# A hybrid block with 256 tokens: 32 tokens of the expert layer by gathered rows, 224 densely, with GpSimd making three units in four of the values' low parts

## The chip, the cores and the metric

The kernel runs on one core of one Trainium2 chip. The metric is the device time of one execution in microseconds (us); lower is better. The engines are TensorE (PE, with its weight loads as PEld), VectorE (DVE), ScalarE (ACT), GpSimd (POOL) and SyncE (SP), which issues the DMAs.

## The reference

One transformer block in float32: a retention branch, an RWKV branch, a merge, then the expert layer ("PEER"), which the change is about. Each of the 256 tokens scores 2 x 128 keys in 8 heads, takes 16 experts of 16384 per head with softmax gates, and sums the experts' outputs:

```python
def block(args):
    xb, eb, gb = args
    ue = jnp.take(expert_u, eb, axis=0)
    act = jax.nn.gelu(jnp.einsum('nhkd,nd->nhk', ue, xb), approximate=False) * gb
    return jnp.einsum('nhk,nhkd->nd', act, jnp.take(expert_v, eb, axis=0))
```

`expert_u` and `expert_v` are 16384 x 2048, 134 MB each. The result is added to the block's input and normalized.

## The kernel before

The expert layer is computed densely. All of both expert matrices streams through, and every expert is computed for every token; a gate of zero removes those that a token did not pick.

Weights come in units of 128 x 1024 (512 KB) into four slots of `raw`. ScalarE makes of each half unit (512 columns) a high part `w_hi` in the fp32r type (helper `hi`, L901), and VectorE or GpSimd makes the low part `w_lo`, which is raw minus high (helper `lo`, L1335 on VectorE, L1323 on GpSimd). `w_hi` and `w_lo` have two slots, used in turn. TensorE multiplies high by high and low activations, and low by high activations.

The first expert stage, called U here (functions `um` and `u_blocks`), has 64 turns of four units k = 0 to 3, two blocks of 128 experts. A unit is eight pairs of matmuls (`mm2`, L470 and L472): weights `w_hi` against 512 columns (256 tokens, high and low), and `w_lo` against 256. `U_SPLIT`'s forerunners `POOL_SLOTS, DVE_SLOTS = (0, 2, 3), (1,)` say who makes the low parts. While U runs, VectorE picks the experts of each token (`pick_steps`), adds the two halves of the sums (`usum`), and ScalarE applies the gelu. In the last 32 turns gates are made too: VectorE builds one-hot rows, ScalarE scales them, TensorE multiplies them (`gates_mm`, L827) and VectorE multiplies them in (`gate_in`, `late_in`, L1886).

The second stage, called V here (`vm`, `v_piece`, `v_blocks`), runs twice over all experts, once for each half of the 2048 output columns (h = 0, 1), 128 units each. The activations of 128 experts are the stationary operand and the weights move: per half unit and per group of 128 tokens three matmuls of 512 columns (L858 to L860). ScalarE copies the activations' high part (L1241), after waiting for the whole of the unit before last, and then makes the unit's two high weight parts:

```python
act.wait_ge(S["half_used"], u * 2 - 2)
act.activation(act_hi[:, k % 2, :], ...).then_inc(S["act2_hi"], 1)
for hh in range(2):
    hi(it + (V0 + h * BLOCKS) // 4, k, hh)
```

VectorE makes the activations' low part (L1968) and all low weight parts. The end adds the stored input, squares, scales and stores.

Of the kernel before, what the change touches and what calls it, by code (L numbers as in the profile page):

```python
# [5 lines left out]
P = 128  # L6
TOK = 256
# [34 lines left out]
POOL_SLOTS, DVE_SLOTS = (0, 2, 3), (1,)  # L42
# [15 lines left out]
EXP_AT, PICKED_AT, GATE_AT = 21, 23, 31  # L58

EARLY = 2 * GATE_AT  # L60
GATE_TURNS = TOK // 8
# [29 lines left out]
def hybrid_block_kernel(nc, a):  # L91
# [4 lines left out]
    with ctx:  # L96
# [153 lines left out]
        late_out = [cst[:, SIN:SIN + TOK], extra[:, 768:1024]]  # L250
# [54 lines left out]
        def u_split_sem(it, k, halves):  # L305

            if k in DVE_SLOTS:
                return S["u_dve"], it * (2 * len(DVE_SLOTS)) + (2 * DVE_SLOTS.index(k) + halves)
            return S["u_pool"], it * (2 * len(POOL_SLOTS)) + (2 * POOL_SLOTS.index(k) + halves)
# [6 lines left out]
        def _(sp):  # L316
# [94 lines left out]

            def load_u(it):
                for k in range(4):
                    if isinstance(it, int) and it == 0:
                        sp.wait_ge(S["unit_split"], 2 * (U0 + k) - 6)
                    else:
                        sp.wait_ge(*u_split_sem(it - 1, k, 2))
                    sp.dma_start(raw[:, k, :], a["peer_u_t"][ds(it * 2 + k // 2, 1), k % 2]
                                 .rearrange("a p n -> p (a n)")).then_inc(S[f"raw_in{k}"], 16)
            run_loop(sp, 0, BLOCKS // 2, load_u)  # L420

            for h in range(2):
                def load_v(it):
                    for k in range(4):
                        if h == 0 and isinstance(it, int) and it == 0:
                            sp.wait_ge(*u_split_sem(BLOCKS // 2 - 1, k, 2))
                        else:
                            sp.wait_ge(S["unit_split"], it * 8 + (2 * (U0 + h * BLOCKS + k) - 6))
# [4 lines left out]
                else:  # L433
                    run_loop(sp, 0, 10, load_v)

                    sp.wait_ge(S["half_used"], 2 * (V0 + BLOCKS + 24))
                    for piece in range(12):
                        load_v(10 + piece)
# [7 lines left out]
                    with sp.Fori(22, BLOCKS // 4) as it:  # L446
                        load_v(it)
# [10 lines left out]
        def _(pe):  # L458
# [7 lines left out]
            def mm2(bank, wh, wl, kc, start, stop):  # L466
# [342 lines left out]
            def um(it, k):  # L809

                for hh in range(2):
                    pe.wait_ge(*u_split_sem(it, k, hh + 1))
# [3 lines left out]
                    for c in range(4):  # L816
                        kc = (k % 2) * 8 + 4 * hh + c
                        cols = slice((4 * hh + c) * P, (4 * hh + c + 1) * P)
                        last = mm2(4 + k // 2, w_hi[:, k % 2, cols], w_lo[:, k % 2, cols], kc, kc == 0, kc == 15)
# [33 lines left out]
            def v_piece(h, k, hh, tt, start, stop):  # L853
                out = PS[:, 4 * h + 2 * tt + hh, :]
                cols = slice(hh * 512, (hh + 1) * 512)
                ah = act_hi[:, k % 2, tt * P:(tt + 1) * P]
                al = act_lo[:, k % 2, tt * P:(tt + 1) * P]
                pe.matmul(out, ah, w_hi[:, k % 2, cols], start=start, stop=False)  # L858
                pe.matmul(out, ah, w_lo[:, k % 2, cols], start=False, stop=False)  # L859
                return pe.matmul(out, al, w_hi[:, k % 2, cols], start=False, stop=stop)  # L860

            def vm(h, it, k, start=False, stop=False):
                u = it * 8 + 2 * (U0 + h * BLOCKS + k)
                pe.wait_ge(S["act2_split"], it * 4 + (h * BLOCKS + k + 1))
                for hh in range(2):
                    pe.wait_ge(S["unit_split"], u + hh + 1)
                    for tt in range(2):
                        last = v_piece(h, k, hh, tt, start, stop)
                    last.then_inc(S["half_used"], 1)

            def last_units():

                for k, tt, hh in ((2, 0, 0), (2, 0, 1), (2, 1, 0), (3, 0, 0), (3, 0, 1), (3, 1, 0), (2, 1, 1), (3, 1, 1)):
                    if tt == 0:
                        pe.wait_ge(S["act2_split"], 2 * BLOCKS - 4 + k + 1)
                        pe.wait_ge(S["unit_split"], 2 * (U0 + 2 * BLOCKS - 4 + k) + hh + 1)
                    last = v_piece(1, k, hh, tt, False, k == 3)
                    if k == 3:
# [1184 lines left out]
```

## Time and profile before

| what | value |
|---|---|
| median of 3 runs | 2414.7 us (2414.02 to 2414.74) |
| the profiled execution | 2414.85 us |
| its span in the profile | 2412.7 us |
| mean granted TensorE clock | 0.997 |

The span runs from the first to the last instruction of the profile. Busy times of the engines overlap. Matmuls are pipelined, so the distance from start to start of two matmuls is what one costs.

### The profile page before, as it was taken

How to read it: one execution, taken by the hardware profiler on the slowest of the kernel's cores; microseconds unless marked ns; L12 is line 12 of the kernel's file. 1: busy time of each engine (PE TensorE's matmuls, PEld its weight loads, DVE VectorE, ACT ScalarE, POOL GpSimd, SP SyncE). 2: the span in 40 equal slices, each digit the busy share in tenths (PEclk: the TensorE clock that was granted, in tenths of full speed). 3: DMA queues.
4: the chain of work that ended last, by engine and by line, in shares of the span. 5: the costliest groups of instructions: out<-in, count | busy, mean ns of one | idle time of the engine just before them, and what ended most of it. 6: DMA issues, size and time to landing. Idle time of an engine off the chain costs nothing.

```text
span 2412.7 us, 43151 instructions
## 1 busy us (share of the span) xinstructions
PE 2382.4 (99%) x13978; PEld 2036.8 (84%) x13978; DVE 1500.4 (62%) x2694; ACT 1363.9 (57%) x2511; POOL 534.4 (22%) x414
## 2 busy tenths in 40 slices
PE   9999999999999999999999999999999999999998
PEld 8888788978888888888888888888888888888886
DVE  5568988476565655767445555555566666666666
ACT  5456544355544545777776666666555555555555
POOL 0000201100000004666666565565100000000000
PEclk9999999999999999999999999999999999999999
DMA  7665553056656565656565555555556555566654
GB/s 217 185 194 147 166 172 125 21 153 196 193 191 213 164 185 192 189 183 184 186 186 166 168 162 158 169 160 158 184 194 195 192 191 192 193 198 221 213 192 165
DMA packets 187075, 429.09 MB, mean 178 GB/s; under 512 B 13173, under 2 KB 81271, under 8 KB 186103
## 3 DMA queue, kind: packets, MB, share of 16 engines
q1 hardware_dynamic: 186999, 428.07, 57.2%
q8 instruction: 49, 0.80, 0.1%
q14 instruction: 27, 0.22, 0.0%
HBM read 423.82 MB, written 4.19 MB: 177 GB/s over the span
## 4 chain that ended last, share of the span: by engine, by line
PE 64%; issue 25%; POOL 6%; DVE 3%; ACT 1%; DMA 0%; POOLq 0%; ACTq 0%; SPq 0%
PE PS L470 20%; PE PS L858 10%; PE PS L860 10%; PE PS L859 10%; PE PS L472 9%; POOL w_lo L1323 5%; PE PS L827 2%; PE PS L513 1%; PE PS L515 1%; PE PS L514 1%; POOL big L1295 1%; PE PS L469 1%; DVE w_lo L1335 1%; DVE inv L1562 0%; PE PS L463 0%
## 5 line engine op out<-in xcount | busy, mean ns | idle before, releaser
L901 ACT ACTIVATE w_hi<-raw 128x512 fp32r<-128x512 f32 x1576 | 953.8, 626 | 566.5 <-PE PS L472 283.2
L470 PE MATMUL PS<-act_both,w_hi 128*128 128x512 f32 x3104 | 1097.2, 399 | 7.1 <-DVE w_lo L1335 6.1
L1335 DVE TENSOR_TENSOR w_lo<-raw,w_hi 128x512 fp32r<-128x512 f32 x1192 | 790.6, 689 | 448.4 <-ACT w_hi L901 445.8
L472 PE MATMUL PS<-act_both,w_lo 128*128 128x256 f32 x2910 | 815.6, 280 | 0.0
L470 PEld LDWEIGHTS PS<-act_both,w_hi 128*128 128x128 f32 x3104 | 577.5, 188 | 135.5 <-DVE w_lo L1335 7.9
L1323 POOL TENSOR_TENSOR w_lo<-raw,w_hi 128x512 fp32r<-128x512 f32 x384 | 496.7, 1312 | 765.6 <-ACT w_hi L901 755.8
L472 PEld LDWEIGHTS PS<-act_both,w_lo 128*128 128x128 f32 x2910 | 550.1, 189 | 4.4 <-issue 0.2
L858 PE MATMUL PS<-w_hi,act_both 128*128 128x512 f32 x1024 | 398.5, 389 | 1.7 <-DVE w_lo L1335 1.7
L859 PE MATMUL PS<-w_lo,act_both 128*128 128x512 f32 x1024 | 398.4, 389 | 0.0
L860 PE MATMUL PS<-w_hi,act_both 128*128 128x512 f32 x1024 | 398.4, 389 | 0.0
L1241 ACT ACTIVATE act_both<-big 128x256 fp32r (+1 forms) x256 | 106.9, 417 | 319.0 <-PE PS L860 317.3
L1968 DVE TENSOR_TENSOR act_both<-big,act_both 128x256 fp32r<-128x256 f32 x256 | 108.8, 425 | 258.0 <-ACT act_both L1241 258.0
L513 PE MATMUL PS<-w_hi,act_both 128*128 128x512 f32 x576 | 226.8, 394 | 2.2 <-DVE w_lo L1335 2.1
L858 PEld LDWEIGHTS PS<-w_hi,act_both 128*128 128x128 f32 x1024 | 192.2, 188 | 42.1 <-DVE act_both L1968 2.1
L860 PEld LDWEIGHTS PS<-w_hi,act_both 128*128 128x128 f32 x1024 | 192.2, 188 | 40.0
L859 PEld LDWEIGHTS PS<-w_lo,act_both 128*128 128x128 f32 x1024 | 192.2, 188 | 39.9
L515 PE MATMUL PS<-w_hi,act_both 128*128 128x512 f32 x576 | 224.3, 389 | 0.0
L514 PE MATMUL PS<-w_lo,act_both 128*128 128x512 f32 x576 | 224.2, 389 | 0.0
L513 PEld LDWEIGHTS PS<-w_hi,act_both 128*128 128x128 f32 x576 | 108.1, 188 | 27.6 <-DVE w_lo L1335 4.9
L514 PEld LDWEIGHTS PS<-w_lo,act_both 128*128 128x128 f32 x576 | 108.2, 188 | 22.5 <-issue 0.5
L515 PEld LDWEIGHTS PS<-w_hi,act_both 128*128 128x128 f32 x576 | 108.1, 188 | 22.5
L1195 ACT ACTIVATE cst<-cst,extra 128x128 f32<-128x128 f32 x256 | 81.0, 387 | 0.0
(238 smaller groups left out, 1494.8 us busy)
## 6 DMA issues: line engine op xcount, KB each, us to landing
raw<-in_peer_u_t SPq DMA_DIRECT2D x256, 512.0 KB, 3.5
raw<-in_peer_v SPq DMA_DIRECT2D x256, 512.0 KB, 4.2
raw<-in_w_in SPq DMA_DIRECT2D x180, 512.0 KB, 3.7
raw<-in_w_out SPq DMA_DIRECT2D x32, 512.0 KB, 4.1
raw<-in_peer_w_q SPq DMA_DIRECT2D x32, 512.0 KB, 4.4
raw<-in_w_ret_branch SPq DMA_DIRECT2D x16, 512.0 KB, 4.3
raw<-in_w_rwkv_branch SPq DMA_DIRECT2D x16, 512.0 KB, 4.7
big<-in_x SPq DMA_DIRECT2D x2, 1024.0 KB, 6.1
```

The costliest lines, as they stand in the source:

```text
L470: last = pe.matmul(PS[:, bank, :], wh, act_both[:, kc, :, :].rearrange("p w n -> p (w n)"), start=start, stop=stop)
L472: last = pe.matmul(PS[:, bank, 0:TOK], wl, act_hi[:, kc, :], start=False, stop=False)
L513: pe.matmul(out, ah, w_hi[:, slot % 2, cols], start=first, stop=False)
L514: pe.matmul(out, ah, w_lo[:, slot % 2, cols], start=False, stop=False)
L515: last = pe.matmul(out, al, w_hi[:, slot % 2, cols], start=False, stop=last_k)
L858: pe.matmul(out, ah, w_hi[:, k % 2, cols], start=start, stop=False)
L859: pe.matmul(out, ah, w_lo[:, k % 2, cols], start=False, stop=False)
L860: return pe.matmul(out, al, w_hi[:, k % 2, cols], start=False, stop=stop)
L901: act.activation(w_hi[:, slot % 2, hh * 512:(hh + 1) * 512], raw[:, slot, hh * 512:(hh + 1) * 512], ACT.Copy).then_inc(S["unit_hi"], 1)
L1323: pool.tensor_tensor(w_lo[:, k % 2, cols], raw[:, k, cols], w_hi[:, k % 2, cols].bitcast(f32), ALU.subtract).then_inc(S["u_pool"], 1)
L1335: dve.tensor_tensor(w_lo[:, slot % 2, cols], raw[:, slot, cols], w_hi[:, slot % 2, cols].bitcast(f32), ALU.subtract).then_inc(S[done], 1)
L1968: dve.tensor_tensor(act_lo[:, k % 2, :], g, act_hi[:, k % 2, :].bitcast(f32), ALU.subtract).then_inc(S["act2_split"], 1)
```

## The change

32 tokens of 256 are taken out of the dense computation. For them the rows of `peer_u` and `peer_v` that they picked are gathered: 32 tokens x 128 picks are 4096 rows, in 32 tiles of 128 rows x 8 KB for each matrix. GpSimd issues an indirect DMA for each tile, two turns ahead of its use. VectorE multiplies a tile of U rows by the tokens and adds up along the row (two instructions of 128x1024), and adds a tile of V rows, times its gate, into `sparse_out` (two more). The tiles of U come at turns 16 to 33 and then at every second turn; those of V at 32 of the 64 turns of V.

The dense part has 224 tokens (`DT`). In both stages a unit is now eight pairs of a 448- and a 224-column matmul (`mm_dense`). In V the values are the stationary operand, so the sums stand with output columns as rows, and TensorE turns them back after each half. The results of the first half and of the 32 tokens are added to the stored input in DRAM by accumulating DMAs that GpSimd issues and waits for. The picks of the first token tile come earlier, those of the second later. The number of gate turns is 28. In V GpSimd makes the low parts of units 0, 1 and 3 and VectorE of unit 2.

```diff
-POOL_SLOTS, DVE_SLOTS = (0, 2, 3), (1,)
+U_SPLIT = {"p_split": (0, 2, 3), "d_split": (1,)}
+V_SPLIT = {"p_split": (0, 1, 3), "d_split": (2,)}
-EXP_AT, PICKED_AT, GATE_AT = 21, 23, 31
+SPARSE = 32
+DT = TOK - SPARSE
+GATE_TURNS = DT // 8
+FIRST_EXP_AT, EXP_AT, PICKED_AT, GATE_AT = 11, 28, 30, UPAIRS - 1 - GATE_TURNS
+PICK_TILES = TOPK * 8 * SPARSE // P
+DOT_AT = [16 + t for t in range(18)] + [GATE_AT + 2 * t for t in range(PICK_TILES - 18)]
+MAC_AT = [66 + 8 * t // 5 for t in range(17)] + [100 + 5 * t // 4 for t in range(PICK_TILES - 17)]
+USED_AT = DOT_AT + MAC_AT
...
+            def mm_dense(bank, wh, wl, both, start, stop):
+                hi_part = both[:, 0, :]
+                if stop:
+                    pe.matmul(PS[:, bank, 0:DT], wl, hi_part, start=False, stop=False)
+                last = pe.matmul(PS[:, bank, 0:2 * DT].rearrange("p (w n) -> p w n", w=2), wh, both, start=start, stop=stop)
+                if not stop:
+                    last = pe.matmul(PS[:, bank, 0:DT], wl, hi_part, start=False, stop=False)
+                return last
...
-            def v_piece(h, k, hh, tt, start, stop):
-                out = PS[:, 4 * h + 2 * tt + hh, :]
-                cols = slice(hh * 512, (hh + 1) * 512)
-                ah = act_hi[:, k % 2, tt * P:(tt + 1) * P]
-                al = act_lo[:, k % 2, tt * P:(tt + 1) * P]
-                pe.matmul(out, ah, w_hi[:, k % 2, cols], start=start, stop=False)
-                pe.matmul(out, ah, w_lo[:, k % 2, cols], start=False, stop=False)
-                return pe.matmul(out, al, w_hi[:, k % 2, cols], start=False, stop=stop)
+            def v_tile(k, j, start, stop):
+                cols = slice(j * P, (j + 1) * P)
+                return mm_dense(j, w_hi[:, k % 2, cols], w_lo[:, k % 2, cols], act2[:, k % 2], start, stop)
...
+            def low_parts(stage, it, of, m):
+                for k in of["p_split"]:
                     for hh in range(2):
+                        pool.wait_ge(S["unit_hi"], 8 * m + (2 * k + hh + 1))
                         cols = slice(hh * 512, (hh + 1) * 512)
                         pool.tensor_tensor(w_lo[:, k % 2, cols], raw[:, k, cols], w_hi[:, k % 2, cols].bitcast(f32),
+                                           ALU.subtract).then_inc(S["p_split"], 1)
+            def gather(t):
+                if t == 0:
+                    pool.wait_ge(S["ids_in"], 16 * 8)
+                if t >= LANDS:
+                    pool.wait_ge(S["used"], 2 * (t - LANDS) + 2)
+                if t >= PICK_TILES:
+                    pool.wait_ge(S["used"], 2 * PICK_TILES)
+                rows, lands = (a["peer_u"][0], land_u) if t < PICK_TILES else (a["peer_v"][0], land_v)
+                j = t % PICK_TILES
+                pool.indirect_dma_start(lands[t % LANDS], None, rows, bass.IndirectOffsetOnAxis(ap=ids[:, j:j + 1], axis=0)).then_inc(S[f"landed{t % LANDS}"], 16)
+            def add_rows(n):
+                pool.wait_ge(S["rows_dve"], 2)
+                pool.wait_ge(S["rows_act"], 2)
+                for tt in range(2):
+                    pool.dma_start(x1_dram[tt * P:(tt + 1) * P, 0:1024], out_rows[:, tt, :], accum_op=ALU.add).then_inc(S["rows_added"], 16)
+                pool.wait_ge(S["rows_added"], 32)
+            def add_sparse():
+                pool.wait_ge(S["used"], 4 * PICK_TILES)
+                for q in range(4):
+                    pool.dma_start(x1_dram[0:SPARSE, :], sparse_out[32 * q:32 * q + 32, :], accum_op=ALU.add).then_inc(S["rows_added"], 16)
+                    pool.wait_ge(S["rows_added"], 16 * (3 + q))
+            for g in range(2 * UPAIRS):
+                for t in range(2 * PICK_TILES):
+                    if USED_AT[t] - 2 == g:
+                        gather(t)
+                if g == 96:
+                    for c in (1, 3, 5, 7):
+                        pool.wait_ge(S["odd_read"], c // 2 + 1)
+                        pool.tensor_tensor(out_T[:, c, SPARSE:TOK], odd_tiles[:, c // 2, 0, :], odd_tiles[:, c // 2, 1, :], ALU.add).then_inc(S["out_odd"], 1)
+                low_parts("u" if g < UPAIRS else "v", g % UPAIRS, U_SPLIT if g < UPAIRS else V_SPLIT, U0 // 4 + g)
+                if g == 96:
+                    add_rows(g)
+                if g == ADD_AT:
+                    add_sparse()
...
+            def sparse_step(g, w):
+                if g not in USED_AT:
+                    return
+                t = USED_AT.index(g)
+                j, half = t % PICK_TILES, slice(1024 * w, 1024 * w + 1024)
+                if w == 0:
+                    dve.wait_ge(S[f"landed{t % LANDS}"], 16 * (t // LANDS + 1))
+                if t < PICK_TILES:
+                    row = land_u[t % LANDS][:, half]
+                    dve.tensor_tensor_reduce(row, row, xw[:, half], 1.0, 0.0, ALU.mult, ALU.add, dots[:, w, j:j + 1]).then_inc(S["used"], 1)
+                    return
+                row = land_v[t % LANDS][:, half]
+                if j == 0:
+                    dve.tensor_scalar(sparse_out[:, half], row, dots[:, 1, j:j + 1], None, ALU.mult).then_inc(S["used"], 1)
+                else:
+                    dve.wait_ge(S["used"], 2 * t + w - 1)
+                    dve.scalar_tensor_tensor(sparse_out[:, half], row, dots[:, 1, j:j + 1], sparse_out[:, half], ALU.mult, ALU.add).then_inc(S["used"], 1)
```

## Rows read from the trace of the kernel before

**Rows 1.** The page: engines, busy us (share of the span) and instructions
```profile
span 2412.7 us, 43151 instructions
...
PE 2382.4 (99%) x13978; PEld 2036.8 (84%) x13978; DVE 1500.4 (62%) x2694; ACT 1363.9 (57%) x2511; POOL 534.4 (22%) x414
```

**Rows 2.** Timeline, first matmul of U, first and last of V: start, duration, instruction
```profile
929.71 0.48 PE L470 MATMUL PS<-act_both,w_hi 128*128 128x512 f32 x1
...
1704.87 0.40 PE L858 MATMUL PS<-w_hi,act_both 128*128 128x512 f32 x1
...
2403.02 0.39 PE L860 MATMUL PS<-w_hi,act_both 128*128 128x512 f32 x1
```

**Rows 3.** Timeline of V, all engines, around the start of one unit
```profile
2000.36 0.39 PE L860 MATMUL PS<-w_hi,act_both 128*128 128x512 f32 x1
...
2000.58 0.39 PE L858 MATMUL PS<-w_hi,act_both 128*128 128x512 f32 x1
...
2000.81 0.39 PE L859 MATMUL PS<-w_lo,act_both 128*128 128x512 f32 x1
...
2000.89 0.42 ACT L1241 ACTIVATE act_both<-big 128x256 fp32r x1 [1.27 <-PE PS L860]
...
2001.21 1.14 ACT L901 ACTIVATE w_hi<-raw 128x512 fp32r<-128x512 f32 x2
...
2001.44 0.42 DVE L1968 TENSOR_TENSOR act_both<-big,act_both 128x256 fp32r<-128x256 f32 x1 [1.02 <-ACT act_both L1241]
...
2001.86 1.29 DVE L1335 TENSOR_TENSOR w_lo<-raw,w_hi 128x512 fp32r<-128x512 f32 x2
```

**Rows 4.** Timeline of U, TensorE: a gate group and pairs behind it
```profile
1299.73 1.05 PE L827 MATMUL PS<-cst 128*128 128x128 f32 x8
...
1301.21 0.28 PE L472 MATMUL PS<-act_both,w_lo 128*128 128x256 f32 x1
1301.32 0.39 PE L470 MATMUL PS<-act_both,w_hi 128*128 128x512 f32 x1
1301.56 0.27 PE L472 MATMUL PS<-act_both,w_lo 128*128 128x256 f32 x1
...
1302.94 0.27 PE L472 MATMUL PS<-act_both,w_lo 128*128 128x256 f32 x1
```

**Rows 5.** Timeline of U, GpSimd, ScalarE and VectorE
```profile
918.01 2.55 POOL L1323 TENSOR_TENSOR w_lo<-raw,w_hi 128x512 fp32r<-128x512 f32 x2 [478.91 <-ACT w_hi L901]
...
919.26 1.30 POOL L1323 TENSOR_TENSOR w_lo<-raw,w_hi 128x512 fp32r<-128x512 f32 x1
...
1508.40 0.63 ACT L901 ACTIVATE w_hi<-raw 128x512 fp32r<-128x512 f32 x1
...
1509.11 2.74 POOL L1323 TENSOR_TENSOR w_lo<-raw,w_hi 128x512 fp32r<-128x512 f32 x2 [0.22 <-ACT w_hi L901]
...
1509.03 0.41 DVE L1886 TENSOR_TENSOR big<-big,cst 128x256 f32 x1
```

**Rows 6.** Timeline, TensorE's first matmuls after a wait for a low part
```profile
250.51 0.50 PE L470 MATMUL PS<-act_both,w_hi 128*128 128x512 f32 x1 [1.04 <-DVE w_lo L1335]
...
250.85 0.28 PE L472 MATMUL PS<-act_both,w_lo 128*128 128x256 f32 x1
```

**Rows 7.** Timeline at the start: GpSimd's memset and SyncE's DMA issues
```profile
0.74 1.80 POOL L1285 MEMSET inv<- 128x2048 f32 x1 [0.29 <-POOLq L2050]
0.74 0.88 SPq L318 DMA_DIRECT2D big<-in_x  x2
```

**Rows 8.** Timeline at the end, VectorE's instruction of 128x1024
```profile
2406.24 1.28 DVE L1999 SCALAR_TENSOR_TENSOR big<-big,small 128x1024 f32<-128x1024 f32 x1
```

**Rows 9.** The page's DMA issues: KB each, us from issue to landing
```profile
raw<-in_peer_u_t SPq DMA_DIRECT2D x256, 512.0 KB, 3.5
...
big<-x_scratch SPq DMA_DIRECT2D x8, 256.0 KB, 4.6
```

**Rows 10.** Windows, a stretch of V: busy us of each engine, TensorE's granted clock, DMA share, GB/s
```profile
2000.00:2200.00 200.00, 200.00 (x884) 165.62 (x883) 124.35 (x220) 107.11 (x221) 0.00 (x0) 1.00 0.61 198
```

More of the change, by code:

```diff
@@ L445, in _ @@
                                          a["final_norm_w"][q * 512:(q + 1) * 512].partition_broadcast(P)).then_inc(S["fw_in"], 16)
-                    with sp.Fori(22, BLOCKS // 4) as it:
+                    for it in range(FINAL_AT + 6, BLOCKS // 4):
                         load_v(it)
@@ new lines, in vm @@
+                    for j in range(4 * hh, 4 * hh + 4):
+                        if start and h == 0:
+                            if j in (4, 5):
+                                pe.wait_ge(S[f"gelu{j - 4}"], 2 * UPAIRS - 1)
+                            if j in (6, 7):
+                                pe.wait_ge(S[f"gated{j - 6}"], GATE_TURNS)
+                        if start and h == 1 and j >= 4:
+                            pe.wait_ge(S["rows_act" if j % 2 else "rows_dve"], (j - 4) // 2 + 1)
+                        last = v_tile(k, j, start, stop)
+                        if stop and j % 4 < 3:
+                            last.then_inc(S["tile_done"], 1)
@@ new lines, in last_units, with turn_last @@
+            def last_units():
+                def turn_last(c):
+                    pe.wait_ge(S["out_even"], 4 + max(c + 1, 2 if c < 4 else 4))
+                    turn_rows(c, 0)
+                for c in range(8):
+                    for k in (2, 3):
+                        if c == 0:
+                            pe.wait_ge(S["act2_split"], 2 * BLOCKS - 4 + k + 1)
+                        if c % 4 == 0:
+                            pe.wait_ge(*split_done("v", BLOCKS // 2 - 1, k, c // 4 + 1))
+                        last = v_tile(k, c, False, k == 3)
+                    last.then_inc(S["tile_done"], 1)
+                    if c >= 2:
+                        turn_last(c - 2)
+                turn_last(6)
+                turn_last(7)
@@ L1219, in u_turn, with top_exp @@
                             hot_gate(i, 1)
-            run_loop(act, 0, EXP_AT, u_blocks)
-            for tt in range(2):
+            def top_exp(tt):
                 act.wait_ge(S["topm"], tt + 1)
                 act.activation(big[:, 94 + tt, 0:P], big[:, 94 + tt, 0:P], ACT.Exp).then_inc(S["gexp"], 1)
+            run_loop(act, 0, FIRST_EXP_AT, u_blocks)
+            top_exp(0)
+            with act.Fori(FIRST_EXP_AT, EXP_AT) as it:
+                u_blocks(it)
+            top_exp(1)
             with act.Fori(EXP_AT, GATE_AT) as it:
@@ L1937, in _ @@
                 at, end = (EARLY + (BLOCKS - EARLY) * m // turns for m in (n, n + 1))
-                last = dve.memset(Z(at, end), 1.0)
+                last = dve.memset(G[:, at:end, :], 1.0)
             link(last)
@@ L1985, in add_last @@
+            dve.wait_ge(*split_done("u", UPAIRS - 1, 3, 2))
+            for h in range(2):
+                for it in range(BLOCKS // 4):
+                    v_lo(h, it)
             def add_last(tt, hh):
-                dve.wait_ge(S["v_done"], 2 * tt + hh + 1)
+                dve.wait_ge(S["rows_T"], 8 + 4 * hh + 4)
                 x1 = flat(Z(8 * tt + 4 + 2 * hh, 8 * tt + 6 + 2 * hh))
-                dve.tensor_tensor(x1, x1, PS[:, 4 + 2 * tt + hh, :], ALU.add).then_inc(S["res_done"], 1)
+                dve.tensor_tensor(x1, x1, PS[:, 2 * hh + tt, :], ALU.add).then_inc(S["res_done"], 1)
@@ L2000, in finish @@
                                          flat(Z(20, 24)), ALU.mult, ALU.mult).then_inc(S["y_ready"], 1)
-            add_last(0, 0)
+            for c in range(8):
+                dve.wait_ge(S["tile_done"], 6 + c + 1)
+                sum_tile(c)
+                if c == 5:
+                    add_last(0, 0)
+            add_last(1, 0)
             add_last(0, 1)
-            add_last(1, 0)
             mean_last(0)
```

243 lines of the change are left out of this document (155 added, 88 removed).

## The prediction

> **What bounds the kernel now.** I read the page's busy shares first [rows 1]: TensorE is busy 99% of the span, VectorE 62%, GpSimd 22%. A busy TensorE is not a TensorE at its peak, so I looked next at how its stages run. The expert stages are a first one (hidden values, "U", 256 units of 512 KB) and a second one (values, "V", 256 units). The timeline puts U from 929.71 to 1704.87 and V from there to 2403.02 [rows 2]: 775.2 us and 698.2 us, together 61% of the span. Everything the change touches lies there.
>
> In V one unit is twelve 512-column matmuls; the reader is to see starts 0.227 us apart with no gap [rows 3], 2.72 us a unit, and 256 x 2.727 is the whole stage. So TensorE's issue is the limit, not a wait. In U a unit is eight pairs of a 512- and a 256-column matmul; five pairs take 1.73 us at the row's place [rows 4]. Over the whole stage I take the gate matmuls out: eight starts in 0.78 us after the first, 0.111 each, 0.89 a group, 1.8 a turn with two groups, 57 us for 32 turns. The rest is 718 us, 2.80 us a unit, 0.350 a pair.
>
> **The change, part by part.**
>
> *Narrower matmuls.* 224 tokens are done densely instead of 256, so a pair is 448 and 224 columns in both stages. Proportional scaling would give 0.350 x 0.875 = 0.306 us. I don't take it: the 128-column matmuls, half as wide as the narrow one now, still start 0.111 us apart, and the 256-column ones take 0.11 (1301.21 to 1301.32) [rows 4]. Something that doesn't shrink with the columns, the weight load by its look, sets a floor near 0.11. So only the wide matmul gains, 64 columns: (0.24 - 0.11) us for 256 more columns [rows 4] is 0.5 ns a column or less, and by the 512-column spacing 0.227/512 [rows 3] it is 0.44; I take 0.027 us a pair. A pair is then 0.323, a unit T = 2.58 (bounds: 2.45 proportional, 2.60). U: 256 x (2.80 - 2.58) = -56 us, and four gate turns fewer, -7. V: its unit of twelve wide matmuls becomes eight pairs with sixteen weight loads, 256 x (2.727 - 2.58) = -38 us. Together -101 us if nothing waits.
> The Trainium skill (TensorE: Matmul & The Clock Gate, LDWEIGHTS) gives a weight load as its columns divided by 1.2 GHz, 107 ns for 128; the rows' 0.111 agrees, and it speaks against the proportional sum, by which the two stages would save another 67 us.
>
> *Low parts on GpSimd in V.* Before, VectorE makes all of V's low parts: 0.69 us each, 0.60 apart [rows 3]. GpSimd takes 1.30 each, 1.25 apart [rows 5], and gets three units in four: 6 x 1.25 = 7.5 us of a group of four units, 10.3 us. As a sum it fits. As a chain it doesn't quite. In V ScalarE's copy of the activations waits for the whole of unit u-2, and the high parts are queued behind it. From the start of unit u-1 to the first matmul of unit u: 0.31 to ScalarE's start (2000.58 to 2000.89), 0.29 for the shorter copy (0.32 for 256 columns), 0.71 from the high part's start to GpSimd's (1508.40 to 1509.11), 1.30, and about 0.10 because the load of the next low weights is exposed after a wait (0.34 between the first two matmuls instead of 0.24) [rows 3, 5, 6]. That is L = 2.71 against T = 2.58. By VectorE it is 2.04 (0.65 and 0.69 for the 0.71 and 1.30), which is why V doesn't wait now. In U the high part waits only for the same half of unit u-2 and no copy stands before it, so 1.5 T = 3.9 is available for some 2.4, and it is hidden.
> GpSimd is also slowed by VectorE: beside a 0.41 us subtraction with both inputs in SBUF (L1886) two low parts take 2.74 us instead of 2.55, +0.19 [rows 5]. V's subtraction for the activations (224 columns, +0.16) falls on the second low part of every GpSimd unit, which is then 0.12 later than its half needs. So GpSimd units last 2.70. Start times in a group, each the later of "previous one's end" and "end of u-2 plus L": k=1 at 0, k=2 at 2.70, k=3 at 5.41, k=0 at 8.11, k=1 at 10.82, against 10.32: 0.50. VectorE's own two low parts, 0.37 each where they fall on GpSimd's, add some; I take 0.7 in all. 64 groups: +45 us (bounds: 0, if the signals are quicker than here, to 1.2 a group, +77).
> The Trainium skill (GPSIMD Engine Reference, Specifications) says that GpSimd's SBUF interface is shared with VectorE and contended by VectorE instructions with two SBUF inputs; the rows of L1886 agree with their 0.19 us, and without that sharing this term would be 28 us less and the next up to 48.
>
> *The gathered tokens in V.* 32 gathers (128 rows of 8 KB, 1 MB) go on GpSimd's queue just ahead of unit k=0's low parts, in 32 of the 64 groups, and VectorE does two multiply-adds of 128x1024 in those groups. No DMA from GpSimd is in this trace. Bounds of what one costs GpSimd: SyncE issues 128 rows of 8 KB in 0.44 us (0.88 for two), and GpSimd's memset of 128x2048, the same tile, takes 1.80 [rows 7]; I take 1.0, in between. A multiply-add has two SBUF inputs, 1.28 us [rows 8], four times the columns of L1886's, so up to 4 x 0.19 = 0.75 us of GpSimd, and both come in GpSimd's units. Sum 2.5 us; the VectorE unit k=2 lets GpSimd catch up by some 0.7; 1.8 x 32 = +58 us (bounds +14, the issue alone, and +106, all of 2.5 and the dearer gather).
> V in all: -38 + 45 + 58 = +65 us.
>
> *The gathered tokens in U.* 18 groups in a row and 14 of the gate turns take a gather and two multiply-reduces. GpSimd has 7.5 + 2.5 = 10.0 us of work in 10.3, with 1.3 us of slack in the chain: I take 0.6 lost in each of the 18, +11, and 0.1 in the 14 longer turns, +1 (bounds 0 and +40). U in all: -56 - 7 + 12 = -51.
>
> *Moves at the edges.* [...] GpSimd then waits for two accumulating DMAs, and at group 119 for four in series, of 256 KB; what is queued behind is the low parts, and TensorE waits for those. 256 KB take 4.6 us from issue to landing [rows 9]. The first wait costs about 4, the four 18 less some slack, but half as likely as not they are quicker than a load; I take 11 (bounds 6 and 18). At the end 16 more transposes and one more add behind the last tile: +4. The earlier picks, the exponentials and the scaling of rows lie beside VectorE's idle 38% and ScalarE's and cost nothing; without that cover they would be a few us. Edges: +23.
>
> **Sum.** -51 + 65 + 23 = +37, and I add 5 for DMA crowding in the 18 groups (next part): +42. Span 2412.7 + 42 = 2455. The profiled execution took 2414.85, 2.1 above its span, and the median of the runs is 2414.7, so the same offset gives 2457.
>
> **Rivals.**
> *GpSimd keeps up (faster).* A gather costs GpSimd 0.44, the multiply-adds slow it little because they fall in its idle time, and the chain just fits. V loses 13 + 14 instead of 103 and stays at -11; U -61; edges 12: -60, 2355. It decides from the point where V's waits come to less than 61 us instead of 103, since the rest of the sum is then zero. For it: 7.5 of 10.3 us, and in U GpSimd waits for ScalarE, not TensorE for it. Against: in V the chain, not the sum, counts. Chance 0.20.
> *The narrow matmul has no floor.* T = 2.45, U gains 33 more; V gains nothing, since L stays and T falls under it. 2424. Against: 0.111 at 128 columns. Chance 0.07.
> *Gathers are dear.* At 1.8 us or more each, and with the accumulating DMAs at 4.6: +26 in V, +14 in U, +7 at the edges: 2504. Chance 0.18.
> *The DMA engines are the bound in U.* At 198 GB/s they are busy 0.61 [rows 10], about 325 at full. 18 groups move 3.15 MB each in 10.3 us, 306 GB/s, so a load that takes 3.5 us now [rows 9] lands late. If no more than 260 can be had, a group takes 12.1: +27 more, 2484. The other groups ask for 267 at most. Chance 0.08, the forecast 0.47.
>
> **Numbers.** Slower holds the forecast, the dear gathers, the DMA case and the no-floor case, 0.80 in all, of which I give back 0.05 for their lower tails: within 0.2%, 5 us (about what these runs can tell from no change), is a thin edge between cases, 0.04, and faster gets 0.21. The likeliest case's own range is 2430 to 2490; the range asked for goes from inside the faster case to the dear one, 2375 to 2510.
>
> **What would show it.** In V of the changed kernel: pairs of 0.32 us, TensorE waiting for w_lo of GpSimd about once a unit, groups near 11.0 us without a gather and near 12.8 with one; GpSimd's mean low part above 1.40 us; V near 763 us, U near 724. In U the narrow slot at 0.11, not 0.10. Wrong if V's groups are 10.3 us with no wait for GpSimd, if a gather takes GpSimd under 0.3 or over 2.5 us, or if VectorE's multiply-adds leave GpSimd's 1.30 as it is.

## The result: 5.6% slower

The changed kernel takes 2549.17 us (2547.04 to 2551.07, 4 runs) against 2414.36 us for the kernel before: ratio 1.0559 [1.054, 1.0577]. The prediction had the direction and put the time at 2457, with a range up to 2510. The time is 92 us above the one and 39 above the other.

The page of the changed kernel, the rows that answer to [rows 1]:

```profile
span 2545.2 us, 43408 instructions
...
PE 2323.8 (91%) x14970; PEld 2061.1 (81%) x14970; DVE 1628.4 (64%) x2477; ACT 1345.4 (53%) x2495; POOL 1177.8 (46%) x872
```

TensorE was busy 99% of its span and is now busy 91%: it waits. The timeline gives the same three marks as [rows 2], first matmul of U, first and last of V:

```profile
927.67 0.45 PE L524 MATMUL PS<-act_both,w_hi 128*128 128x448 f32 x1
...
1694.37 0.84 PE L524 MATMUL PS<-act_both,w_hi 128*128 128x448 f32 x2
...
2532.66 0.38 PE L524 MATMUL PS<-act_both,w_hi 128*128 128x448 f32 x1
```

The middle row holds U's last matmul and V's first, which starts at 1694.77. So U is 767.1 us (775.2 before), V 837.9 (698.2), and behind the last matmul stand 12.5 us (9.7). With 2.0 us gained ahead of U the span grows by -2.0 - 8.1 + 139.7 + 2.9 = 132.5: it is all in V. U is only 8 us shorter, so it gave back nearly all that the narrower matmuls saved there.

What TensorE waits for, the view of waits (engine, line, releaser: us in all, times, longest):

```profile
PEld PS L524 <- POOL w_lo L1426: 215.4, 246, 22.1
...
PE PS L524 <- POOL w_lo L1426: 144.0, 125, 21.8
...
PE PS L524 <- DVE act_both L2146: 39.3, 31, 1.3
```

L1426 is GpSimd's low part. L2146 is VectorE's subtraction that makes the activations' low part (L1968 before). 39.3 us in 31 waits, 1.27 us each, for an instruction of 0.39 us is odd; what lengthens it is looked into below.

I call a turn the four units of both stages (U 0 to 63, V 64 to 127), measured from first matmul to first matmul:

| turn | predicted | measured |
|---|---|---|
| U, nothing beside it | 10.32 | 10.05 |
| U with a tile (17 to 22; over all of 16 to 33 it is +2.0) | +0.6 | +1.9 |
| U with gates | +1.8 | +1.78 |
| U with gates and a tile | +0.1 more | +2.34 more |
| V without a tile | 11.0 | 10.55 |
| V, each tile | +1.8 | +3.7 |

The last row is from turns 67 to 90, 12.86 us on average with 15 tiles in 24 turns: (12.86 - 10.55) x 24/15 = 3.7.

**What a tile does.** I call the work on one gathered tile a tile for short: a gather on GpSimd, and two turns later two wide VectorE instructions. A stretch of V with a tile, from the timeline in three windows, GpSimd and VectorE alone (start, duration, instruction, and in brackets the idle time before it):

```profile
1927.53 1.36 POOL L1426 TENSOR_TENSOR w_lo<-raw,w_hi 128x512 fp32r<-128x512 f32 x1
...
1927.66 2.31 DVE L2055 SCALAR_TENSOR_TENSOR big<-inv,vec,big 128x1024 f32<-128x1024 f32 x1
...
1928.86 2.26 POOL L1426 TENSOR_TENSOR w_lo<-raw,w_hi 128x512 fp32r<-128x512 f32 x1
...
1929.90 1.46 DVE L2146 TENSOR_TENSOR act_both<-big,act_both 128x224 fp32r<-128x224 f32 x1
...
1931.28 1.28 DVE L1478 TENSOR_TENSOR w_lo<-raw,w_hi 128x512 fp32r<-128x512 f32 x2
...
1937.51 0.95 POOL L1439 DMA_INDIRECT inv<-in_peer_v,vec  x1 [0.15 <-issue]
...
1938.48 4.99 POOL L1426 TENSOR_TENSOR w_lo<-raw,w_hi 128x512 fp32r<-128x512 f32 x4
...
1939.49 4.24 DVE L2146 TENSOR_TENSOR act_both<-big,act_both 128x224 fp32r<-128x224 f32 x1 [3.28 <-ACT act_both L1338]
```

Read the ends. GpSimd's low part ends at 1928.89. VectorE's multiply-add (L2055) started at 1927.66, 0.13 after it, and ends at 1929.97, 1.08 after the low part's end: it needs 1.28 alone [rows 8], so it did nearly all its work after GpSimd's. The next low part starts at 1928.86 and ends at 1931.12, 1.15 after the multiply-add's end, of 1.29 that one takes alone: again nearly its whole work behind the other's. L2146 starts at 1929.90 and ends at 1931.36, behind that low part. The two engines take turns, and the recorded durations hold the waits. At 1939.49, behind the gather, L2146 starts while a low part runs and ends at 1943.73, when four low parts have run (1938.48 to 1943.47). VectorE's low part (L1478), 1.28 for two at 1931.28, runs with GpSimd idle.

Over the whole run: 156 of the 256 L2146 start inside a low part. 125 of them end soon after the end of that low part (lengthened by about what was left of it: 0.34 to 0.49 us for the 64 that start 0.45 to 0.70 us before its end), and 31 are lengthened by 3.8 us (median).

### The profile page after: what moved, and what is told of

It is laid out like the page before. It is cut to its first block, busy times and chain, and to the rows that moved or that the text cites. A ratio compares the mean times of both kernels' runs of the same rounds, so it can differ in the third digit from the quotient of the medians.

```text
span 2545.2 us, 43408 instructions
## 1 busy us (share of the span) xinstructions
PE 2323.8 (91%) x14970; PEld 2061.1 (81%) x14970; DVE 1628.4 (64%) x2477; ACT 1345.4 (53%) x2495; POOL 1177.8 (46%) x872
## 4 chain that ended last, share of the span: by engine, by line
PE 63%; DVE 14%; POOL 11%; ACT 5%; issue 4%; DMA 2%; ACTq 1%; SPq 0%; DVEq 0%; POOLq 0%
PE PS L524 21%; POOL w_lo L1426 10%; PE PS L526 9%; PE PS L514 9%; DVE act_both L2146 5%; PE PS L567 5%; PE PS L569 5%; PE PS L568 5%; PE PS L516 4%; ACT w_hi L986 3%; PE PS L507 3%; DVE w_lo L1478 2%; PE PS L881 1%; DVE big L2048 1%; DMA x_scratch<-big 1%
## 5 line engine op out<-in xcount | busy, mean ns | idle before, releaser
L524 PE MATMUL PS<-act_both,w_hi 128*128 128x448 f32 x4096 | 1347.4, 383 | 186.3 <-POOL w_lo L1426 144.0
L1426 POOL TENSOR_TENSOR w_lo<-raw,w_hi 128x512 fp32r<-128x512 f32 x768 | 1071.2, 1423 | 924.6 <-ACT w_hi L986 913.9
L526 PE MATMUL PS<-act_both,w_lo 128*128 128x224 f32 x3952 | 1050.0, 266 | 0.0
L524 PEld LDWEIGHTS PS<-act_both,w_hi 128*128 128x128 f32 x4096 | 770.0, 189 | 307.5 <-POOL w_lo L1426 215.4
L1478 DVE TENSOR_TENSOR w_lo<-raw,w_hi 128x512 fp32r<-128x512 f32 x808 | 602.2, 766 | 402.9 <-ACT w_hi L986 401.2
L526 PEld LDWEIGHTS PS<-act_both,w_lo 128*128 128x128 f32 x3952 | 757.9, 192 | 0.6
L2146 DVE TENSOR_TENSOR act_both<-big,act_both 128x224 fp32r<-128x224 f32 x256 | 264.5, 1037 | 394.5 <-ACT act_both L1338 394.5
L514 PE MATMUL PS<-act_both,w_hi 128*128 128x512 f32 x1056 | 372.0, 399 | 8.1 <-DVE w_lo L1478 6.6
L516 PE MATMUL PS<-act_both,w_lo 128*128 128x256 f32 x990 | 277.8, 281 | 0.0
L514 PEld LDWEIGHTS PS<-act_both,w_hi 128*128 128x128 f32 x1056 | 196.4, 188 | 56.8 <-DVE w_lo L1478 8.8
L567 PE MATMUL PS<-w_hi,act_both 128*128 128x512 f32 x576 | 226.8, 394 | 2.2 <-DVE w_lo L1478 2.1
L569 PE MATMUL PS<-w_hi,act_both 128*128 128x512 f32 x576 | 224.3, 389 | 0.0
L568 PE MATMUL PS<-w_lo,act_both 128*128 128x512 f32 x576 | 224.2, 389 | 0.0
L516 PEld LDWEIGHTS PS<-act_both,w_lo 128*128 128x128 f32 x990 | 187.0, 189 | 1.4 <-issue 0.2
L567 PEld LDWEIGHTS PS<-w_hi,act_both 128*128 128x128 f32 x576 | 108.1, 188 | 27.6 <-DVE w_lo L1478 4.9
L569 PEld LDWEIGHTS PS<-w_hi,act_both 128*128 128x128 f32 x576 | 108.1, 188 | 22.5
```

Of the source, the lines that this page charges most:

```text
L514: last = pe.matmul(PS[:, bank, :], wh, act_both[:, kc, :, :].rearrange("p w n -> p (w n)"), start=start, stop=stop)
L524: last = pe.matmul(PS[:, bank, 0:2 * DT].rearrange("p (w n) -> p w n", w=2), wh, both, start=start, stop=stop)
L526: last = pe.matmul(PS[:, bank, 0:DT], wl, hi_part, start=False, stop=False)
L567: pe.matmul(out, ah, w_hi[:, slot % 2, cols], start=first, stop=False)
L568: pe.matmul(out, ah, w_lo[:, slot % 2, cols], start=False, stop=False)
L569: last = pe.matmul(out, al, w_hi[:, slot % 2, cols], start=False, stop=last_k)
```

## Experiments

The kernel before ran on the same chip beside each group: 2413.9 us beside the four kernels of experiments 1 and 2, 2413.8 beside those of 3, 4, 6 and 7, 2412.2 beside that of 5.

**1. VectorE makes all low parts of V.**

```diff
-V_SPLIT = {"p_split": (0, 1, 3), "d_split": (2,)}
+V_SPLIT = {"p_split": (), "d_split": (0, 1, 2, 3)}
```

> The changed kernel with all of V's low parts on VectorE again (GpSimd only gathers there). Exclusion theory (a GpSimd instruction and a VectorE instruction with two SBUF inputs never run together, each waits for the other, so their times add): the sum falls from about 12.9 us a turn with a gathered tile to 3.2, VectorE's own work is 8.6 us, so TensorE sets the turn at 10.05 us; V falls from 838 us to about 670 and the time to about 2375. If the gathers' traffic on the DMA engines holds V up: turns with a tile stay above 12 us, time above 2490. If only the longer chain through GpSimd counts and the gathered work is as dear as before: V falls by the 0.5 us of a turn without a tile, 30 us, time about 2515.

2383.73 us (2381.63 to 2385.18), ratio 0.9875 [0.9858, 0.9891]: without GpSimd's share in V the changed kernel is 1.2% faster than the kernel before, and that share costs 165 us. V's turns take 10.03 us, 10.17 in the stretch with tiles. Groups of the changed kernel, then of this one (busy us, mean ns):

```profile
L2146 DVE TENSOR_TENSOR act_both<-big,act_both 128x224 fp32r<-128x224 f32 x256 | 264.5, 1037 | 394.5 <-ACT act_both L1338 394.5
```

```profile
L2146 DVE TENSOR_TENSOR act_both<-big,act_both 128x224 fp32r<-128x224 f32 x256 | 100.1, 391 | 120.8 <-ACT act_both L1338 120.3
```

The same 256 instructions take 164 us less where GpSimd makes no low part beside them. The windows of V, changed kernel (1710 to 2090), then this one (1710 to 1950); the columns are those of [rows 10]:

```profile
1710.00:2090.00 380.00, 327.64 (x1940) 289.74 (x1939) 214.63 (x217) 172.98 (x363) 269.69 (x198) 1.00 0.62 211
```

```profile
1710.00:1950.00 240.00, 237.91 (x1511) 225.79 (x1510) 187.81 (x313) 136.57 (x284) 19.14 (x14) 1.00 0.79 267
```

VectorE is busy 78% of this stretch and TensorE 99%; GpSimd does the gathers alone. The granted clock is 1.00, the 2.4 GHz level, in both, so the clock has no part in this stretch (experiment 5 has the two longest stretches of U and V in which it fell).

**2. The sparse part taken apart.** Three variants of the changed kernel. *One input*: VectorE's multiply-reduce and multiply-add are replaced by a sum along the same row (1024 columns, one SBUF input), so the sparse results are lost. *Gather only*: that sum over one column. *No gather*: only the first tiles of each matrix are gathered, VectorE's work stays as it was on what they left, without waiting for more.

```diff
-dve.tensor_tensor_reduce(row, row, xw[:, half], 1.0, 0.0, ALU.mult, ALU.add, dots[:, w, j:j + 1])
+dve.tensor_reduce(dots[:, w, j:j + 1], row, AX.X, ALU.add)                # one input; gather only: row[:, 0:1]
-dve.scalar_tensor_tensor(sparse_out[:, half], row, dots[:, 1, j:j + 1], sparse_out[:, half], ALU.mult, ALU.add)
+dve.tensor_reduce(dots[:, 0, (2 * j + w) % 32:(2 * j + w) % 32 + 1], row, AX.X, ALU.add)
...
-                    if USED_AT[t] - 2 == g:
+                    if USED_AT[t] - 2 == g and t % PICK_TILES < LANDS:    # no gather
```

> The changed kernel with the multiply-reduces and multiply-adds replaced by sums along the same 128x1024 rows, one input in SBUF, about the same length (their results are not the gathered tokens'). Exclusion theory: these no longer hold GpSimd up nor wait for it; the cost of a gathered tile falls from 3.7 to about 1.2 us in V and from 2 to under 1 in U, time about 2440. If VectorE's busy time or its order is what costs: no change, 2549. If the DMA traffic costs: no change either.

> The changed kernel with those VectorE instructions cut to one column (the gathered tokens are not computed), all gathers kept. Exclusion theory: what is left of a tile is GpSimd's 0.95 us; 1.0 to 1.4 us in V, 0 to 0.5 in U, time about 2430. DMA theory: a tile keeps its 3.7 us, 2549.

> The changed kernel with all of the VectorE work on the gathered rows but only the first three gathers of each matrix (the rest of the rows is stale). Exclusion theory: a tile falls by the gather's 0.95 us in V, to about 2.7, less in U; time about 2505. DMA theory: a tile costs next to nothing, time about 2400.

One run of each: 2476.91, 2457.97 and 2469.12 us. All three expectations were off, by +37, +28 and -36 us, and the turns say where (us; U's plain turns with a tile are the mean of turns 17 to 22, in brackets of all 18; gate turns are medians; V per tile over a turn of 10.55, from turns 67 to 90):

| | U turn with a tile | gate turn with a tile | V per tile |
|---|---|---|---|
| changed kernel | 11.95 (12.03) | 14.17 | 3.7 |
| no gather | 10.98 (11.32) | 13.16 | 2.0 |
| one input | 10.92 (10.87) | 13.27 | 2.3 |
| gather only | 10.58 (10.55) | 12.21 | 2.3 |
| no tile | 10.05 | 11.83 | 0 |

In V one input and gather only are the same, 2.3: two VectorE instructions of 1.21 us that read one SBUF tensor cost nothing there. With two inputs they cost 2.0 a tile where nothing is gathered, and 3.7 - 2.3 = 1.4 on top of a gather. So what matters in V is the second SBUF input, and the gather has a price of its own, 2.3 us for an instruction of 0.95 (next experiment). In U the one-input sums aren't free: 0.3 us in a plain turn and 13.27 - 12.21 = 1.06 in a gate turn. VectorE's own time seems to count there, apart from GpSimd; no run separates it.

GpSimd's low parts, changed kernel, then gather only:

```profile
L1426 POOL TENSOR_TENSOR w_lo<-raw,w_hi 128x512 fp32r<-128x512 f32 x768 | 1071.2, 1423 | 924.6 <-ACT w_hi L986 913.9
```

```profile
L1426 POOL TENSOR_TENSOR w_lo<-raw,w_hi 128x512 fp32r<-128x512 f32 x768 | 987.0, 1313 | 918.6 <-ACT w_hi L986 907.3 <-DMA x_scratch<-big 8.3
```

GpSimd loses 84 us to VectorE's wide instructions, 0.11 a low part. That is close to what I had predicted, 128 instructions of 0.75 = 96. The long subtractions are another matter, as gather only shows, where no wide instruction is left:

```profile
L2146 DVE TENSOR_TENSOR act_both<-big,act_both 128x224 fp32r<-128x224 f32 x256 | 271.5, 1065 | 428.8 <-ACT act_both L1338 428.8
```

271.5 us against 264.5 in the changed kernel, and again 31 of them over 3 us: what lengthens them is GpSimd's low parts, above all behind a gather, not the multiply-adds.

**3. The gather in another place.** In V it is issued between GpSimd's units 1 and 3, where VectorE makes unit 2 and GpSimd has a pause, instead of ahead of unit 0.

```diff
                 for k in of["p_split"]:
+                    if stage == "v" and k == 3:
+                        gathers_of(m - U0 // 4)
```

> The changed kernel with V's gathers issued between GpSimd's units 1 and 3, while VectorE's unit 2 runs, not ahead of unit 0. If a gather costs because it stands ahead of a low part in a chain without slack: a tile falls from 3.7 us to about 2.3, time about 2505. If what costs is the sum of the times that exclude each other: the place does not matter, 2549 within 10.

2497.86 us (1 run), 51 less. A turn with only the gather now takes 10.54 us, as one without, and one with the multiply-adds 12.46. The subtraction's line in V of the changed kernel, and in V of this one (both from 1700 to 2080 us):

```profile
L2146 DVE TENSOR_TENSOR act_both<-big,act_both 128x224 fp32r<-128x224 f32 x121 | 131.9, 1095 | 164.6 <-ACT act_both L1338 164.6
```

```profile
L2152 DVE TENSOR_TENSOR act_both<-big,act_both 128x224 fp32r<-128x224 f32 x130 | 91.9, 707 | 186.8 <-ACT act_both L1338 186.8
```

So the 2.3 us of a gather in V are its own 0.95, because GpSimd's chain has no slack ahead of unit 0, and 1.3 for the subtraction that then stands behind four low parts in a row: TensorE's waits for L2146 above are 31 of 1.27 us, for 32 tiles. With the gather moved the longest subtraction takes 1.47 us, and the waits for it are gone. Moved, the gather is free in V. A tile costs 12.46 - 10.55 = 1.9 us there.

**4. The split alone, in the kernel before.** Its V gets GpSimd for units 0, 1 and 3; nothing else changes.

```diff
+V_POOL, V_DVE = (0, 1, 3), (2,)
...
+            with pool.Fori(0, BLOCKS // 2) as it:
+                for k in V_POOL:
+                    for hh in range(2):
+                        pool.wait_ge(S["unit_hi"], it * 8 + (2 * (V0 + k) + hh + 1))
```

> The kernel before with only the last words of the change: in V GpSimd makes the low parts of units 0, 1 and 3, VectorE of unit 2; 256 tokens, moving weights, nothing gathered. Exclusion theory: GpSimd 7.5 us and VectorE's subtractions 1.2 and 1.2 us are 9.9 us of a turn of 10.9, so the sum fits and only the chain counts, whose 2.74 us stand against a unit of 2.73; a wait of 0 to 0.5 us a turn, time 2415 to 2445, VectorE's subtraction for the activations (L1975 here) up from 425 to about 750 ns. If the split by itself were what made the changed kernel slow (its V costs 2.4 us a turn more than its matmuls): over 2480.

2429.28 us (2428.74 to 2430.74), ratio 1.0065 [1.0048, 1.0082]; V's turns take 11.03 us against 10.88. The time is in the range, the subtraction isn't at the 750 ns expected:

```profile
L1981 DVE TENSOR_TENSOR act_both<-big,act_both x256: 416/468/823, 1703.7 to 2412.2; 128x256 fp32r<-128x256 f32 x128
```

(shortest, median, longest in ns.) Without gathers and wide multiply-adds the two engines meet little, and the chain costs 0.15 us a turn of 10.88. The split by itself is a small loss; it becomes a large one with what the change adds beside it.

**5. The four accumulating DMAs of turn 119.** The changed kernel's GpSimd, timeline:

```profile
2419.96 0.89 POOL L1452 DMA_DIRECT2D x_scratch<-big  x1
2424.26 0.79 POOL L1452 DMA_DIRECT2D x_scratch<-big  x1 [3.41 <-DMA x_scratch<-big]
2428.50 0.75 POOL L1452 DMA_DIRECT2D x_scratch<-big  x1 [3.46 <-DMA x_scratch<-big]
2432.68 0.76 POOL L1452 DMA_DIRECT2D x_scratch<-big  x1 [3.42 <-DMA x_scratch<-big]
2442.07 3.88 POOL L1426 TENSOR_TENSOR w_lo<-raw,w_hi 128x512 fp32r<-128x512 f32 x3 [8.63 <-ACT w_hi L986]
```

One takes 4.2 us with its wait, but the low parts start again not behind the fourth but 5 us later: SyncE waits for all four as well and loads no weights meanwhile. Its loads restart when the fourth is in, and ScalarE has no unit to split until one has landed, 22 us after its last.

```profile
2436.69 0.34 SPq L471 DMA_DIRECT2D raw<-in_peer_v  x1
...
2441.28 1.15 ACT L986 ACTIVATE w_hi<-raw 128x512 fp32r<-128x512 f32 x2 [21.91 <-DMA raw<-in_peer_v]
```

The experiment leaves the four DMAs out, and with them SyncE's wait for them (it still waits for the two of the first half):

```diff
-                    sp.wait_ge(S["rows_added"], 16 * 6)
+                    sp.wait_ge(S["rows_added"], 16 * 2)
...
-                if g == ADD_AT:
-                    add_sparse()
```

> The changed kernel without its four accumulating DMAs (the last results of the sparse part are then not added to out; everything else is as in the changed kernel). In the changed kernel the turn in which they are issued and the one after took 32.5 and 11.9 us, 23.4 more than two turns of 10.5. If the wait of GpSimd and SyncE for these four transfers, one after the other, is the cause, the two turns are 10.5 to 11 each and the kernel takes about 2526 us, the end behind the last matmul 12 as it was. Rival: the two turns are long for another reason (the stores of the rows just before, or low parts that are late anyway); then most of the 23 us stays and the time is over 2540.

2532.35 us (1 run, before 2412.22). Turns 119 and 120 take 10.5 us each instead of 32.5 and 11.9: 23.4 us, as expected, are theirs, and V's second half is 23.1 shorter (409.7 against 432.8). The span falls by only 14.7 us, since U (769.5 against 767.1), V's first half (407.6 against 405.1) and the rest are longer in this one run, places that the edit doesn't touch. The cause holds; the total was missed by 6. GpSimd's wait and SyncE's were taken away together, so the run doesn't say which is worth how much.

The granted clock has a small part here: behind the two longest stops TensorE started again at the 1.2 GHz level. The windows of the changed kernel, behind the gap between the halves and around turn 119 (columns as in [rows 10]):

```profile
2115.60:2125.80 10.20, 5.56 (x19) 5.17 (x20) 0.00 (x0) 0.38 (x2) 4.96 (x4) 0.50 0.46 116
2426.20:2446.70 20.50, 3.31 (x11) 3.10 (x12) 0.84 (x1) 2.47 (x5) 6.14 (x6) 0.50 0.63 167
```

TensorE stood still for 10.0 and 22.1 us before its first matmul in them. The 19 and 11 matmuls run at 0.50 took 5.6 and 3.3 us, where 0.157 each, as at 1.00, would be 3.0 and 1.7. So some 1.6 of the 23.4 us, and 2.6 us between the halves, are the clock's.

**6. A better version.** From experiment 1, with U's gathers between GpSimd's units 0 and 2, more V tiles in the first half, and the four DMAs at turn 113.

```diff
-V_SPLIT = {"p_split": (0, 1, 3), "d_split": (2,)}
+V_SPLIT = {"p_split": (), "d_split": (0, 1, 2, 3)}
-MAC_AT = [66 + 8 * t // 5 for t in range(17)] + [100 + 5 * t // 4 for t in range(PICK_TILES - 17)]
+MAC_AT = [66 + 5 * t // 4 for t in range(22)] + [100 + 5 * t // 4 for t in range(PICK_TILES - 22)]
-IDS_AT, ADD_AT, FINAL_AT = 13, 119, 24
+IDS_AT, ADD_AT, FINAL_AT = 13, 113, 24
```

> All of V's low parts on VectorE, U's gathers between GpSimd's units 0 and 2, and V's tiles earlier (22 of 32 in the first half), so that the four accumulating DMAs end long before SyncE waits for them. Expected: the turns 119 and 120 go from 13.7 and 12.9 us to 10.0, 6 to 7 us less; U's plain turns with a tile go from 11.85 to 11.0 if the place of the gather counts (18 turns, 15 us) and stay if the sum does. Time 2362 or 2377.

2346.35 us (2344.99 to 2351.21), ratio 0.9719 [0.9703, 0.9735], faster than both kernels. That is 16 us under the lower of the two expected times. U is 742.5 us (a tile costs 1.1 in a plain turn of 17 to 22, 1.3 in a gate turn), V 663.5. The gate turns with a tile went from 14.17 to 13.17, which I hadn't counted and which is worth 14 us. Its V, 1710 to 1950:

```profile
1710.00:1950.00 240.00, 237.06 (x1503) 224.34 (x1502) 197.49 (x320) 135.86 (x282) 20.90 (x18) 1.00 0.84 286
```

286 GB/s at 10.23 us a turn, nearly as fast as without tiles (10.03): at that rate the DMA engines aren't the bound.

**7. The same remedy in U's gate turns.** Version 6, with VectorE making two units' low parts in four instead of one.

```diff
+G_SPLIT = {"p_split": (0, 2), "d_split": (1, 3)}
...
-            of = U_SPLIT if stage == "u" else V_SPLIT
+            of = {"u": U_SPLIT, "g": G_SPLIT, "v": V_SPLIT}[stage]
```

> As early_mid, and in the 29 last turns of U VectorE makes the low parts of units 1 and 3, GpSimd of 0 and 2. Exclusion theory: of a gate turn with a tile GpSimd's 7.5 us become 5.0 and VectorE's 1.2 become 2.2, 1.5 us less of times that exclude each other, so its 14.17 us fall to about 12.7: 20 us less than early_mid. If VectorE's busy time is what sets these turns (10.2 of 11.8 us): not faster, or slower.

2377.49 us (2376.55 to 2382.14), ratio 0.9856 [0.984, 0.9873]: not 20 us faster but 31 slower than version 6. Gate turns take 12.57 us without a tile (11.83 in version 6) and 14.74 with one (13.17). The windows of the gate turns, version 6, then this one:

```profile
1350.00:1650.00 300.00, 288.87 (x1921) 273.38 (x1921) 216.76 (x336) 185.92 (x433) 213.83 (x156) 1.00 0.60 206
```

```profile
1350.00:1650.00 300.00, 278.46 (x1759) 251.02 (x1759) 251.66 (x353) 160.01 (x396) 144.41 (x99) 1.00 0.54 192
```

VectorE is busy 252 of 300 us. It also adds the sums up (L2029) for which ScalarE's gelu waits:

```profile
ACT extra L1276 <- DVE extra L2029: 70.0, 22, 3.8
ACT cst L1276 <- DVE cst L2029: 70.0, 22, 3.8
```

In version 6's same stretch the first of these is 53.9 us and the second is not among the waits. In V there is no such work, which is why the same remedy helps there. I had carried the result of V over to a stage with another queue; the waits fit that reading, and no run moved the sums in VectorE's order to test it.

## Why the prediction was wrong

**The step that failed** is the price of a tile: "Sum 2.5 us; the VectorE unit k=2 lets GpSimd catch up by some 0.7; 1.8 x 32" in V, and "GpSimd has 7.5 + 2.5 = 10.0 us of work in 10.3, with 1.3 us of slack in the chain", so 0.6 and 0.1 a tile, in U. It reckons with GpSimd's queue alone and counts on slack in it. The runs showed 3.7 us a tile in V and 1.9 and 2.3 in U, because low parts on GpSimd and two-input instructions on VectorE exclude each other in both directions, so that VectorE's instructions wait too and there is no slack.

In V the price of the parts was about right: a gather 0.95 (1.0 taken), the multiply-adds 1.4 us on top of it (2 x 0.75 taken). What was wrong is the 0.7 of catching up, of which nothing came, and a term that wasn't there at all, the 1.3 us for which the activations' subtraction waits behind four low parts. 1.5 + 1.0 + 1.3 is 3.8 against 3.7 measured. That the multiply-adds came out near the 1.5 is partly luck: alone ("no gather" and experiment 3) they cost 1.9 to 2.0.

In U the times of all instructions with two SBUF inputs add up, and the gather to them. In a turn with a tile, by the spacings in the trace: GpSimd's low parts 6 x 1.25 = 7.5, VectorE's 2 x 0.60 = 1.2, its multiply-reduces 2 x 1.14 = 2.3 (1121.76 to 1122.90), and the gather 0.95: 11.95, as turns 17 to 22 have it (12.03 over all 18). I had 10.0, without VectorE's 1.2 and with 1.5 for the 2.3. The same sum for V with the gather moved, with four subtractions of 0.31 (1933.24 to 1933.55), is 7.5 + 1.2 + 2.3 + 1.2 = 12.2 against 12.46 measured. It isn't the whole rule: for a U turn of "one input" it gives 9.65, less than TensorE's 10.05, and the turn took 10.9.

The rows would have told it. In [rows 5] two low parts lost 0.19 us to an instruction that had 0.33 left when the first of them started (1509.11 to 1509.44). In the changed kernel a waiting low part ended 1.15 us behind the other instruction, 0.14 less than the 1.29 it takes alone, and 0.33 - 0.14 is 0.19. So the 0.19 was a wait for what was left, and not a slowing in proportion to the columns.

The Trainium skill (GPSIMD Engine Reference, Specifications) names VectorE instructions with two SBUF inputs among those that contend with GpSimd; the experiments agree: in V 0 us a tile for sums with one input ("one input" against "gather only"), 2.0 for two ("no gather").

The terms by size, from the turns:

- V's tiles: 32 x 3.7 = 118 us, predicted 58. It is the largest miss, +60: 32 x (0.7 + 1.3) = 64, less 0.1 a tile. Alone the multiply-adds cost 2.0 a tile and the gather 2.3; together they cost less than their sum, 3.7.
- U's tiles: 18 x 1.9 + 14 x 2.34 = 67 us, predicted 12: +55.
- Edges: turn 119 and the next +23.4 where I took 11 (bounds 6 and 18). That was 2.75 us a DMA; one takes 4.2, and the restart of SyncE's loads behind the fourth 5 more, with 1.6 for the clock. Between the halves, turns 95 to 97 (13.8, 20.3 and 14.1 us) hold 16.6 over three of 10.55, where I had put 8. Behind the last matmul +2.9, predicted 4. Of these edges, the 4 us for turning the tiles between the halves stand on no run: the changed kernel's 32 transposes are one matmul each, mostly 0.11 us from start to start, 1.7 us for 16. Edges in all 43, predicted 23: +20.
- T: 2.51 us a unit (10.05 / 4), predicted 2.58: -17 us in U. The floor for the narrow matmul was wrong. From start to start the wide one took 0.236 before and 0.211 now, as predicted (0.025 less; 0.027 taken), and the narrow one 0.117 before and 0.102 now, where I had put no gain (means of 1200 to 1300 us before, 950 to 1000 us after). It is shorter by the share of its columns, 224 of 256, and shorter than the 0.111 of the 128-column gate matmuls from which I had read the floor. Neighbouring rows of the changed kernel:

```profile
949.99 0.26 PE L526 MATMUL PS<-act_both,w_lo 128*128 128x224 f32 x1
950.09 0.37 PE L524 MATMUL PS<-act_both,w_hi 128*128 128x448 f32 x1
950.30 0.27 PE L526 MATMUL PS<-act_both,w_lo 128*128 128x224 f32 x1
950.40 0.37 PE L524 MATMUL PS<-act_both,w_hi 128*128 128x448 f32 x1
```

- The chain in V: 10.55 - 10.03 (experiment 1's turn) = 0.5 us a turn. The recurrence gave 0.50 and I took 0.7. The mechanism was right; that the 0.50 came out is partly luck, since with the measured T of 2.51 the same recurrence gives a turn of 10.75, 0.70 over 10.05. By this and T, V's turns are 0.45 under the forecast, -29 us for 64.
- DMA crowding in U, +5: gather only moves 3.15 MB in a turn of 10.58 us, 298 GB/s, and ScalarE waits there for a load 3 times in 13 turns, 3.9 us in all. The changed kernel, slower in those turns, has as little: about as predicted or less.

The differences are +60 + 55 + 20 - 17 - 29 = +89, against 90.5 that the span has more than forecast (132.5 against 42). With these terms U is 64 x 10.05 + 28 x 1.78 + 67 = 760 (measured 767.1; turns 0 to 15 alone are 6 us over 16 of 10.05), and V 64 x 10.55 + 118 + 23 + 17 = 833 (837.9).

**The rivals.** "GpSimd keeps up" (2355) was wrong for the kernel as changed; versions 1 and 6 end near its time, but by keeping GpSimd out of V. "Gathers are dear" named the side, but not the cause: a gather is 0.955 us, and the price lies in what stands beside and behind it. "No floor" had the better reading of the narrow matmul, but not of T (2.45 against 2.51, as far off as my 2.58), and its time, 2424, fell with the price of the tiles. "The DMA engines are the bound" supposed no more than 260 GB/s and is refuted by 298. What no rival had was the subtraction's wait in V and the missing slack; that is why the range ended at 2510.

Of what I had said would show it, these came: waits for w_lo about once a unit, yes; GpSimd's mean low part over 1.40 us, yes (1.423), but this sign was too weak, since it sees one side only. V near 763 and U near 724, and the narrow slot at 0.11 and not 0.10: no (837.9, 767.1, 0.102).

**Left open.** Why 31 of the 156 subtractions are passed over by three more low parts, while the other waiting instructions get in at the end of the running one, no run here shows. It is seen where GpSimd runs four low parts without a pause behind a gather, and not with the gather moved away (longest 1.47 us). Open as well is what one-input sums and a gather cost in U's plain turns, 10.9 and 10.6 us, where the sum of the excluding times leaves room.

## What to carry to other kernels

Before work is moved between VectorE and GpSimd, sum the times of all instructions of both that read two tensors of SBUF, as if they were one engine, and compare that sum with the time per turn. A queue that fits by itself says nothing. Look at the durations on both sides, those of the short instructions above all: 0.39 us that become 4.24 are a wait in disguise. Put what GpSimd must issue, gathers or accumulating DMAs, where its next piece isn't due, and let no engine that feeds TensorE wait for a chain of transfers.

## What the runs showed of the hardware

- A GpSimd and a VectorE instruction that both read two SBUF tensors hardly overlap: one does its work behind the other's end, in either direction (1.29 becomes 2.26 us for GpSimd's, 1.28 becomes 2.31 and 0.39 becomes 4.24 for VectorE's), and the record shows the wait as duration. VectorE's sums over one SBUF tensor, 1.21 us each, leave GpSimd's low parts as they are (mean 1.314 us with them, 1.313 without) and cost V's turns nothing.
- An indirect DMA of 128 rows of 8 KB occupies GpSimd 0.95 us in the changed kernel (shortest, median and longest in ns):

```profile
L1439 POOL DMA_INDIRECT inv<-in_peer_v,vec x22: 948/953/997, 1692.2 to 2359.8; - x22
```

- An accumulating DMA of 256 KB into DRAM takes 4.2 us from its issue to the next one's, which waits for it; 0.8 of that is the issue itself.
- A pair of 448 and 224 columns takes 0.313 us, 0.211 + 0.102, against 0.353 for 512 and 256 columns, 0.236 + 0.117: both matmuls of it got shorter. Matmuls of 128 columns, each with its own weights, start 0.111 apart all the same.
- After TensorE had stood still for 10 and 22 us it ran its first 5.6 and 3.3 us of matmuls at a granted clock of 0.50, the 1.2 GHz level.
